# One GpSimd instruction instead of four, and the sample ranks one step earlier

## The chip, the cores and the metric

The kernel runs on one core of one Trainium2 chip. The metric is the device time of one execution in microseconds. The kernel before was timed three times: 759.83, 761.39 and 762.85 us, median 761.39 us.

## The reference

The kernel computes one inference step of one decoder layer in fp32, for a prompt of 256 tokens and for 8 sample sequences of one new token each with 1024 past positions in a paged cache:

```
x = x + 0.5 * g1 * SwiGLU_1(mod1(rmsnorm(x)))
h = mod2(rmsnorm(x)); [qA|kA|vA|qB|kB|vB|gA|gB] = h @ w_in
  A: block-sparse attention, 8 heads x 64, blocks of 256, top 3 past blocks + own block
  B: differential attention, 4 heads, q/k halves of 64, value 128
x = x + g2 * ((sig(gA) * yA + sig(gB) * yB) @ w_out)
x = x + 0.5 * g3 * SwiGLU_2(mod3(rmsnorm(x)))
```

The part that matters here is the attention of the sample group in branch A. Of the four past blocks of a sequence only three take part: those with the highest mean score. Each block's score is compared with the others' (ties go to the lower block), and a block that has three or more ahead of it is masked. After that comes the softmax over the past keys and the new one.

## The kernel before, in words

The 264 tokens (256 + 8) lie along the free dimension, features on the partitions. A weight block is 128 x 2048 floats. Each is split into a high part (a ScalarE copy to the fp32r format, `hi`, L723) and a low part (`lo`: raw minus high, on VectorE at L1069 or on GpSimd at L674), and each product of 128 x 128 is three matmuls (L1626 to L1628). `hi` and `lo` work on halves of a block, 128 x 1024 elements. The order on each engine is written out by hand, and engines meet through semaphores that only count up.

The change lies in the middle stage, from about 290 to 400 us. There the engines run a loop over steps u. At step u:

- TensorE multiplies half u of the weights for keys and values (`kv_product(u)`, halves 0 to 19; halves 16 to 19 belong to the gates), turns the result of the step before (`v_turn`, L1810 and L1811), then multiplies the sample queries with a block of cached keys: `scores(0, u + 2)` and `scores(1, u)`, L1875. Branch A's blocks come through SP's queue (kvA), branch B's through GpSimd's queue (kvB). After step 16 come halves 17 and 18, the turned probabilities (`turn_probs(0)`, L1919), `block_sums(1)`, half 19, and then the products of probabilities and cached values (PV, L2009), whose progress frees the slots for later loads.
- VectorE turns the cached key blocks in place (`turn_keys(ab, u)`, L1280) before TensorE can use them: `turn_keys(0, u + 3)` and `turn_keys(1, u + 1)`. So key block 15 of branch B is turned at its step 14 and used at TensorE's step 15. Between them it has small work: `place_q` (L1299), the products of new queries and keys (`own_products`, L1308), and for sequences of group 0 `sample_logits(0)` (step 10), a copy of the current scores (`ncur`, L1472, step 13), `sample_ranks(0)` (L1337 to L1362, step 14), `prompt_logits(0)` (step 15), `sample_scale(0)` (step 16). Group 1's `sample_ranks(1)` comes after the loop.
- ScalarE copies each product out of its bank (`v_out`, tile vT, L865, and `v_tokens`), cuts the high part of half u + 3, and at its step 14 does `sample_exp(0)` (L880), which waits for the end of `sample_ranks(0)`.
- GpSimd, for each use of a key/value slot of branch B, issues four loads (`kv_load`, L480), which wait until the slot's earlier content has been used, and then cuts the low part of one half (`lo`, halves 5 to 19, fifteen in all). It also stores rows of keys and values (L656, L657).
- `exp_sums(0)` (L1910) on TensorE adds up the exponentials of group 0 over partitions; `sample_scale(0)` waits for it.

SP loads the weight blocks in program order between its own key/value loads; a raw slot is free when the low part of its last half is cut.

Of the kernel before, what the change touches and what calls it, by code (L numbers as in the profile page):

```python
# [16 lines left out]
F32 = mybir.dt.float32  # L17
F32R = mybir.dt.float32r
I32 = mybir.dt.int32
ALU = mybir.AluOpType  # L20
# [5 lines left out]
KC = D // P  # L26
# [186 lines left out]
def build(nc, A, O):  # L213
    ctx = ExitStack()
    with ctx:
# [17 lines left out]
        raw = [place(f"raw{s}", [P, UNIT]) for s in range(SLOTS)]  # L233
        whi = [place(f"whi{s}", [P, UNIT], F32R) for s in range(2)]
        wlo = [place(f"wlo{s}", [P, UNIT], F32R) for s in range(2)]
# [106 lines left out]
        s_hi, s_lo, s_gemm = sem("hi_ready"), sem("lo_ready"), sem("gemm_done")  # L342
# [88 lines left out]
        def half_view(tensor, key, t):  # L431

            n = key[1]
            nk, w = (KC, 256) if W_FF1 <= n < W_DN1 or W_FF2 <= n < W_DN2 else fixed_block(n)[1:]
            return tensor[:, 0:nk * w].rearrange("p (k n) -> p k n", k=nk)[:, :, t * w // 2:(t + 1) * w // 2]
# [196 lines left out]
        @block.gpsimd  # L632
        def _(pool):
            late = CW["dist"][0]
            pool.dma_start(const[:, 0:late], A["consts"][:, 0:late]).then_inc(s_const, 16)

            pool.wait_ge(s_sil, 1)
            pool.dma_start(const[:, late:NCONST], A["consts"][:, late:NCONST]).then_inc(s_const_late, 16)
            pool.wait_ge(s_gemm, half_done(W_DN1 - 1, 1))
            for e in range(2):  # L640
                pool.dma_start(held_ada[e][:, :], ada_src(3, e)).then_inc(s_held[e], 16)
            pool.wait_ge(s_alo, NPAIR)
            for e in range(2, 8):
                pool.dma_start(held_ada[e][:, :], ada_src(3, e)).then_inc(s_held[e], 16)
            pool.wait_ge(s_gemm, half_done(W_QK - 1, 1))
            pool.wait_ge(s_ptab, 16)
            for use in range(KVS + 2):
                kv_load(pool, 1, use)

            def row_out(name, ab, p, src, srcs, done):  # L650
                c0 = 256 * p
                name += ("_moba", "_diff")[ab]
                dst = O[name + "_prompt"][0, 0].rearrange("(a p) h d -> p a (h d)", p=P)[:, :, c0:c0 + 256]
                dsts = O[name + "_sample"][0, :, 0].rearrange("s h d -> s (h d)")[:, c0:c0 + 256]
                f0 = 512 * ab + c0
                pool.dma_start(dst, src[:, :, f0:f0 + 256]).then_inc(done, 16)  # L656
                pool.dma_start(dsts, srcs[:, f0:f0 + 256]).then_inc(done, 16)  # L657

            K_ROWS = {8: 0, 10: 1, 11: 2, 13: 3}
            V_ROWS = {14: 0, 16: 1, 18: 2, 19: 3}  # L660
            pool.wait_ge(s_ada, ADA_N2 + 4)
            for b in range(2):
                ins = nc.gpsimd.memset(qrow[b][:, :, :], 0.0)
            ins.then_inc(s_qzero, 1)
            def lo(n, t):

                key = ("w", n)
                s = slot_of(key)
                pool.wait_ge(s_raw[s], landed(key))
                pool.wait_ge(s_hi, half_done(n, t))  # L670
                pool.wait_ge(s_lo, half_done(n, t) - 1)
                low, full, high = half_view(wlo[n % 2], key, t), half_view(raw[s], key, t), half_view(whi[n % 2], key, t).bitcast(F32)
                for k in range(0, KC, 2):
                    ins = nc.gpsimd.tensor_tensor(low[:, k:k + 2, :], full[:, k:k + 2, :], high[:, k:k + 2, :], ALU.subtract)  # L674
                ins.then_inc(s_lo, 1)

            for use in range(KVS + 2, 4 * TS):
                kv_load(pool, 1, use)
                if 6 <= use <= 11:
                    lo(*filler(use - 1))  # L680
                if 11 <= use < POOL_HALVES - 1:
                    lo(*filler(use))
                if use == POOL_HALVES - 2:
                    lo(*filler(use + 1))
                if use in K_ROWS:
                    i = K_ROWS[use]
                    pool.wait_ge(s_tok, 4 * (i + 1))
                    row_out("k", i // 2, i % 2, ktok, ktoks, s_krow)
                if use in V_ROWS:
                    i = V_ROWS[use]  # L690
                    pool.wait_ge(s_vtok, 4 * (i + 1))
                    row_out("v", i // 2, i % 2, vtok, vtoks, s_vrow)

            def load_last(e):
                pool.dma_start(ada_dst(last_ada[e], ADAS - 1), ada_src(ADAS - 1, e)).then_inc(s_last[e], 16)

            pool.wait_ge(s_pv, 4 * TS)
            load_last(0)
            pool.wait_ge(s_vrow, 16 * 8)
            pool.wait_ge(s_po, KC)  # L700
            load_last(1)
            pool.wait_ge(s_ext, 3)
            load_last(2)
            load_last(3)
# [354 lines left out]
        def _(v):  # L1059
# [378 lines left out]
            for u in range(2 * TS + 2):  # L1438
                if 2 <= u < 18:
                    kind, i = kv_half(u - 2)  # L1440
                    if kind == "k":
                        k_reciprocals(i)
                if u == 2:
                    lo(*filler(4))
                if u % 2 and u + 3 < 16:
                    place_q(0, (u + 3) // 2)
                if u + 3 < 16:
                    turn_keys(0, u + 3)
                if u % 2 and 4 <= u + 1 < 16:
                    place_q(1, (u + 1) // 2)  # L1450
                if u + 1 < 16:
                    turn_keys(1, u + 1)
                if u == 3:
                    for buf in range(2):
                        ins = dve.memset(wpad[buf][:, :, :, :], 0.0)
                    ins.then_inc(s_wzero, 1)
                if u == 10:
                    v.wait_ge(s_kS[1], GUEST_LAST + 1)
                    for e in range(2):
                        for m in mxt[e]:  # L1460
                            ins = dve.memset(m[:, :], 0.0)
                    ch.link(ins)
                    sample_logits(0)
                if u == 11:
                    own_products()
                if u == 12:
                    prompt_q_roots()
                    v.wait_ge(s_mod, ADAS - 1)
                    coefficients(2, R_N3)
                if u == 13:  # L1470
                    v.wait_ge(s_cur, 1)
                    dve.tensor_copy(ncur[:, :], bank[:, 4, 0:4]).then_inc(s_ncur, 1)  # L1472
                if u == 14:
                    v.wait_ge(s_ncur, 1)
                    sample_ranks(0)
                if u == 15:
                    prompt_logits(0)
                if u == 16:
                    sample_scale(0)
# [138 lines left out]
        def _(pe):  # L1618
# [309 lines left out]
            for u in range(2 * TS + 1):  # L1928
                kv_product(u)
                if 1 <= u < 17:  # L1930
                    kind, i = kv_half(u - 1)
                    if kind == "k":
                        k_sum(i)
                    else:
                        v_turn(u - 1, i)
                if 2 <= u < 18:
                    kind, i = kv_half(u - 2)
                    if kind == "k":
                        k_turn(u - 2, i)
                if 3 <= u < 19:  # L1940
                    kind, i = kv_half(u - 3)
                    if kind == "k":
                        k_back(i)
                if u == 5:
                    pe.wait_ge(s_nvar, 3)
                if u == 13:
                    pe.wait_ge(s_ecur, 1)
                    pe.wait_ge(s_kroot, 8)
                    for r4 in range(4):
                        ins = mm(bank[:, 4, r4:r4 + 1], ev0[:, r4, :], C("ones", 0, 1), start=True, stop=True)  # L1950
                    ins.then_inc(s_cur, 1)
                if u + 2 < 16:
                    scores(0, u + 2)
                if u < 16:
                    scores(1, u)
                if u == 11:
                    block_sums(0)
                if u == 14:
                    pe.wait_ge(s_knorm, 8)
                    pe.wait_ge(s_ncur, 1)  # L1960
                    pe.wait_ge(s_part, 1)
                    prompt_scores(0)
                if u == 16:
                    exp_sums(0)

            def gate_half(s, t):
# [182 lines left out]
```

## Time and profile before

| | value |
|---|---|
| time, median of 3 | 761.39 us |
| profiled execution, its own time | 759.83 us |
| its span, first to last instruction | 758.1 us |
| TensorE / VectorE / ScalarE / GpSimd busy | 730.7 / 462.4 / 333.9 / 130.5 us |
| granted TensorE clock, mean | 0.995 |
| HBM traffic over the span | 275 GB/s |

Busy time is the union of an engine's instructions; matmul ends are modelled, so a busy TensorE need not be at its peak. The idle time before an instruction is put down to the engine or transfer whose signal came last.

### The profile page before, as it was taken

How to read it: one execution, taken by the hardware profiler on the slowest of the kernel's cores; microseconds unless marked ns; L12 is line 12 of the kernel's file. 1: busy time of each engine (PE TensorE's matmuls, PEld its weight loads, DVE VectorE, ACT ScalarE, POOL GpSimd, SP SyncE). 2: the span in 40 equal slices, each digit the busy share in tenths (PEclk: the TensorE clock that was granted, in tenths of full speed). 3: DMA queues.
4: the chain of work that ended last, by engine and by line, in shares of the span. 5: the costliest groups of instructions: out<-in, count | busy, mean ns of one | idle time of the engine just before them, and what ended most of it. 6: DMA issues, size and time to landing. Idle time of an engine off the chain costs nothing.

```text
span 758.1 us, 17337 instructions
## 1 busy us (share of the span) xinstructions
PE 730.7 (96%) x6732; PEld 651.7 (86%) x6732; DVE 462.4 (61%) x699; ACT 333.9 (44%) x568; POOL 130.5 (17%) x224
## 2 busy tenths in 40 slices
PE   5899999999999999999989999999989999999997
PEld 2498998999999699999876666599979999999997
DVE  1764445355454779997998555868675545545451
ACT  1553344334343543554345534565463444444431
POOL 0000000002000231797975233110000000000000
PEclk9999999999999999999999999989999999999999
DMA  8978989997995599999999999985616665554620
GB/s 355 377 256 273 321 296 302 335 286 260 401 303 175 213 398 385 360 397 391 406 391 338 408 402 364 361 301 168 207 35 209 186 197 166 173 191 162 200 79 29
DMA packets 116521, 209.57 MB, mean 276 GB/s; under 512 B 6714, under 2 KB 100186, under 8 KB 104162
## 3 DMA queue, kind: packets, MB, share of 16 engines
q1 hardware_dynamic: 106784, 159.47, 60.8%
q0 software_dynamic: 9440, 49.04, 16.4%
q8 instruction: 47, 0.77, 0.4%
q14 instruction: 24, 0.20, 0.1%
q10 hardware_dynamic: 226, 0.10, 0.0%
HBM read 205.33 MB, written 3.24 MB: 275 GB/s over the span
## 4 chain that ended last, share of the span: by engine, by line
PE 79%; DVE 8%; DMA 7%; issue 2%; ACT 2%; SPq 1%; POOL 0%; ACTq 0%; POOLq 0%; DVEq 0%
PE bank L1626 21%; PE bank L1627 20%; PE bank L1628 20%; PE bank L1682 3%; PE bank L1875 3%; DMA raw<-in_w_in 2%; DMA kvA_lent<-in_cache_v_moba 2%; PE bank L2009 2%; DMA kvA<-in_cache_k_moba 1%; PE bank L1690 1%; DMA const<-in_consts 1%; PE bank L1974 1%; SPq L480 1%; DVE wlo L1069 1%; PE bank L1975 1%
## 5 line engine op out<-in xcount | busy, mean ns | idle before, releaser
L1069 DVE TENSOR_TENSOR wlo<-raw,whi 128x1024 fp32r<-128x1024 f32 (+1 forms) x177 | 208.5, 1198 | 175.8 <-ACT whi L723 172.9
L1626 PE MATMUL bank<-hhi,whi 128*128 128x264 f32 x992 | 286.7, 289 | 5.3 <-DVE wlo L1069 2.6
L1627 PE MATMUL bank<-hlo,whi 128*128 128x264 f32 x992 | 282.0, 284 | 0.0
L1628 PE MATMUL bank<-hhi,wlo 128*128 128x264 f32 x992 | 281.6, 284 | 0.0
L723 ACT ACTIVATE whi<-raw 128x1024 fp32r<-128x1024 f32 (+1 forms) x192 | 194.5, 1034 | 111.2 <-PE bank L1628 83.7
L1626 PEld LDWEIGHTS bank<-hhi,whi 128*128 128x128 f32 x992 | 187.6, 189 | 17.8 <-issue 15.0
L1627 PEld LDWEIGHTS bank<-hlo,whi 128*128 128x128 f32 x992 | 187.7, 189 | 0.1
L1628 PEld LDWEIGHTS bank<-hhi,wlo 128*128 128x128 f32 x992 | 186.8, 188 | 0.0
L1626 PE MATMUL bank<-ahi,whi 128*128 128x264 f32 x416 | 119.8, 288 | 0.4 <-DVE alo L1584 0.4
L1628 PE MATMUL bank<-ahi,wlo 128*128 128x264 f32 x416 | 118.2, 284 | 0.0
L1627 PE MATMUL bank<-alo,whi 128*128 128x264 f32 x416 | 117.6, 283 | 0.0
L1626 PEld LDWEIGHTS bank<-ahi,whi 128*128 128x128 f32 x416 | 78.3, 188 | 0.8 <-DVE alo L1584 0.6
L1627 PEld LDWEIGHTS bank<-alo,whi 128*128 128x128 f32 x416 | 78.3, 188 | 0.2
L1628 PEld LDWEIGHTS bank<-ahi,wlo 128*128 128x128 f32 x416 | 78.3, 188 | 0.0
L757 ACT ACTIVATE sil<-bank 128x528 f32<-128x528 f32 x22 | 13.5, 612 | 73.7 <-PE bank L1628 73.7
L674 POOL TENSOR_TENSOR wlo<-raw,whi 128x256 fp32r<-128x256 f32 x60 | 42.8, 744 | 2.9 <-issue 1.4
L761 ACT ACTIVATE ahi<-act 128x528 f32 (+1 forms) x22 | 14.2, 646 | 53.7 <-DVE act L1155 53.7
L480 POOL DMA_DIRECT2D kvB<-in_cache_v_diff x44 | 23.3, 529 | 40.5 <-PE bank L2009 31.8
L1974 PE MATMUL bank<-hhi,whi 128*128 128x264 f32 x96 | 28.5, 297 | 0.0
L1159 DVE TENSOR_TENSOR alo<-act,ahi 128x528 f32 (+1 forms) x22 | 15.6, 708 | 19.4 <-ACT ahi L761 19.4
L1975 PE MATMUL bank<-hlo,whi 128*128 128x264 f32 x96 | 27.3, 284 | 0.0
L1976 PE MATMUL bank<-hhi,wlo 128*128 128x264 f32 x96 | 27.2, 283 | 0.0
(286 smaller groups left out, 814.7 us busy)
## 6 DMA issues: line engine op xcount, KB each, us to landing
raw<-in_ffn_w_gate SPq DMA_DIRECT2D x22, 1024.0 KB, 5.4
raw<-in_ffn_w_up SPq DMA_DIRECT2D x22, 1024.0 KB, 5.5
raw<-in_w_ada SPq DMA_DIRECT2D x20, 1024.0 KB, 6.9
raw<-in_w_in SPq DMA_DIRECT2D x20, 1024.0 KB, 11.9
raw<-in_ffn_w_down SPq DMA_DIRECT2D x16, 1024.0 KB, 5.0
kvB<-in_cache_v_diff POOLq DMA_DIRECT2D x44, 256.0 KB, 6.3
kvA<-in_cache_v_moba SPq DMA_DIRECT2D x40, 256.0 KB, 8.7
kvA<-in_cache_k_moba SPq DMA_DIRECT2D x36, 256.0 KB, 6.7
```

Source lines behind the costliest of these rows:

```text
L480: eng.dma_start(rows_, cache[bass.ds(page, 1)].rearrange("a (j t) d -> (a j) (t d)", t=4)).then_inc(kv_sem(ab, use), 16)
L674: ins = nc.gpsimd.tensor_tensor(low[:, k:k + 2, :], full[:, k:k + 2, :], high[:, k:k + 2, :], ALU.subtract)
L723: nc.scalar.activation(half_view(whi[key[1] % 2], key, t), half_view(raw[s], key, t), ACT.Copy).then_inc(s_hi, 1)
L1069: dve.tensor_tensor(half_view(wlo[key[1] % 2], key, t), half_view(raw[s], key, t), half_view(whi[key[1] % 2], key, t).bitcast(F32), ALU.su ...
L1626: mm(out, wh, xh, start=start, stop=False)
L1627: mm(out, wh, xl, start=False, stop=False)
L1628: return mm(out, wl, xh, start=False, stop=stop)
L1682: ins = mm(bank[32 * j:32 * j + 32, b, 0:n].rearrange("p (t a) -> p t a", a=32), csilu[:, kc, :], cols[:, :, j, :], start=(kc == 0), stop= ...
L1875: ins = mm(bank[32 * m:32 * m + 32, b6, c0:c0 + 128].rearrange("p (q c) -> p q c", q=4), qrow[s % 2][:, 16 * ab + 4 * m + b, :], kv_slot(a ...
L1974: mm(out, wh, hhi[:, k, :], start=(k == 0), stop=False)
L1975: mm(out, wh, hlo[:, k, :], start=False, stop=False)
L1976: ins = mm(out, wl, hhi[:, k, :], start=False, stop=(k == KC - 1))
```

## The change

In GpSimd's `lo`, the loop over four pieces of 128 x 256 elements becomes one instruction over 128 x 1024. On VectorE, `sample_ranks(0)` moves from the start of what step 14 does at its end to the end of step 13, so it now stands ahead of `turn_keys(1, 15)`, which belongs to step 14. On TensorE, `exp_sums(0)` moves from the end of step 16 to the end of step 15, so ahead of `kv_product(16)` and the `v_turn` of half 15.

```diff
-                low, full, high = half_view(wlo[n % 2], key, t), half_view(raw[s], key, t), half_view(whi[n % 2], key, t).bitcast(F32)
-                for k in range(0, KC, 2):
-                    ins = nc.gpsimd.tensor_tensor(low[:, k:k + 2, :], full[:, k:k + 2, :], high[:, k:k + 2, :], ALU.subtract)
-                ins.then_inc(s_lo, 1)
+                nc.gpsimd.tensor_tensor(half_view(wlo[n % 2], key, t), half_view(raw[s], key, t), half_view(whi[n % 2], key, t).bitcast(F32),
+                                        ALU.subtract).then_inc(s_lo, 1)
...
                 if u == 13:
                     v.wait_ge(s_cur, 1)
                     dve.tensor_copy(ncur[:, :], bank[:, 4, 0:4]).then_inc(s_ncur, 1)
-                if u == 14:
                     v.wait_ge(s_ncur, 1)
                     sample_ranks(0)
...
-                if u == 16:
+                if u == 15:
                     exp_sums(0)
```

## Rows read from the trace of the kernel before

**Rows 1.** The page: busy time, share and instructions of each engine; shares of the chain.
```profile
PE 730.7 (96%) x6732; PEld 651.7 (86%) x6732; DVE 462.4 (61%) x699; ACT 333.9 (44%) x568; POOL 130.5 (17%) x224
...
PE 79%; DVE 8%; DMA 7%; issue 2%; ACT 2%; SPq 1%; POOL 0%; ACTq 0%; POOLq 0%; DVEq 0%
```

**Rows 2.** Waits of TensorE, 340 to 426 us: us in total, times, longest.
```profile
PE bank L1810 <- ACT vT L865: 1.5, 1, 1.5
PE bank L1626 <- POOL wlo L674: 1.2, 1, 1.2
PE bank L2009 <- DMA kvA_lent<-in_cache_v_moba: 1.1, 1, 1.1
PE bank L1875 <- DVE kvB L1280: 0.9, 2, 0.7
PE bank L2009 <- ACT wpad L966: 0.2, 1, 0.2
```

**Rows 3.** Windows: length, busy PE, PEld, DVE, ACT, POOL; clock, DMA share, GB/s.
```profile
372.00:396.00 24.00, 21.34 (x241) 19.42 (x242) 21.60 (x52) 10.04 (x27) 20.80 (x32) 1.00 1.03 400
400.00:408.00 8.00, 8.00 (x97) 3.92 (x90) 7.43 (x20) 3.14 (x12) 4.10 (x8) 1.00 0.81 262
```

**Rows 4.** The chain that ended last, 366 to 412 us: start, us, what.
```profile
377.16 18.67 DMA raw<-in_w_in
...
397.86 0.58 ACT probT L887
```

**Rows 5.** Timeline of VectorE: start, us, instruction, count, idle before and its releaser.
```profile
357.85 1.75 DVE L1299 TENSOR_TENSOR qrow<-qrep,const 128x32 f32<-128x32 f32 x2
...
361.71 0.28 DVE L1299 TENSOR_TENSOR qrow<-qrep,const 128x32 f32<-128x32 f32 x2
...
364.11 1.61 DVE L1308 TENSOR_TENSOR stat<-qT,kT 128x32 f32<-128x32 f32 x2
...
374.52 0.12 DVE L1472 COPY ncur<-bank 128x4 f32<-128x4 f32 x1
375.82 2.31 DVE L1280 STREAM_TRANSPOSE kvB<-kvB 128x2048 f32<-128x2048 f32 x1 [1.18 <-DMA kvB<-in_cache_k_diff]
378.06 0.13 DVE L1337 COPY sm<-bank 128x8 f32<-128x8 f32 x1
...
379.77 0.75 DVE L1350 TENSOR_SCALAR sm<-sm,const 128x8 f32<-128x8 f32 x1
...
382.99 0.54 DVE L1357 TENSOR_TENSOR mxt<-mxt,ncur 128x2 f32<-128x2 f32 x1
...
384.52 0.16 DVE L1362 TENSOR_TENSOR ncur<-ncur,mxt 128x2 f32<-128x2 f32 x1
...
395.62 0.17 DVE L1337 COPY sm<-bank 128x8 f32<-128x8 f32 x1
...
400.20 0.16 DVE L1362 TENSOR_TENSOR ncur<-ncur,mxt 128x2 f32<-128x2 f32 x1
```

**Rows 6.** Timeline of ScalarE, columns as in rows 5.
```profile
384.72 0.51 ACT L880 ACTIVATE prob<-prob,mxt 128x256 f32<-128x256 f32 x1 [6.55 <-DVE ncur L1362]
```

**Rows 7.** Timeline of GpSimd, three of the fifteen low halves.
```profile
356.60 2.80 POOL L674 TENSOR_TENSOR wlo<-raw,whi 128x256 fp32r<-128x256 f32 x4
...
374.89 2.80 POOL L674 TENSOR_TENSOR wlo<-raw,whi 128x256 fp32r<-128x256 f32 x4
...
381.07 3.13 POOL L674 TENSOR_TENSOR wlo<-raw,whi 128x256 fp32r<-128x256 f32 x4
```

**Rows 8.** The page, groups: busy us, mean ns of one; VectorE's low parts.
```profile
L1069 DVE TENSOR_TENSOR wlo<-raw,whi 128x1024 fp32r<-128x1024 f32 (+1 forms) x177 | 208.5, 1198 | 175.8 <-ACT whi L723 172.9
```

**Rows 9.** Timeline of TensorE: scores(1, 15) and the first matmul of half 18.
```profile
380.59 1.08 PE L1875 MATMUL bank<-kvB,qrow 128*32 128x128 f32 x32
...
391.11 0.36 PE L1626 MATMUL bank<-hhi,whi 128*128 128x264 f32 x1 [1.20 <-POOL wlo L674]
```

**Rows 10.** Window, columns as in rows 3.
```profile
494.00:504.00 10.00, 9.78 (x53) 9.55 (x54) 4.53 (x9) 5.62 (x10) 2.15 (x3) 0.66 0.96 361
```

## The prediction, made before the changed kernel ran

> **What bounds the kernel now.** I read the page first: TensorE is busy 730.7 of 758.1 us, and the chain that ended last is TensorE's for 79% [rows 1]. So a change in the other engines counts only where TensorE stands still. The second view is the list of waits between 340 and 426 us: TensorE loses 1.5 us to a copy on ScalarE (vT), 1.2 us to a low half from GpSimd, 0.9 us in two waits for a turned key block, 0.2 us for the padded weights and 1.1 us for a transfer [rows 2]. These are all the gains that this stretch can give. The third view, the windows, shows who is short of time there: from 372 to 396 us VectorE is busy 21.6 of 24 us and the DMA engines are full (share 1.03); from 400 to 408 us their share falls to 0.81 [rows 3]. The chain of waits passes this place not through TensorE at all, but through an 18.67 us transfer of input weights that lands at 395.83 us, two copies on ScalarE and the turned probabilities at 397.86 us [rows 4].
>
> The 1.5 us wait arises so. VectorE's copy of the current scores is done at 374.6 us; then it waits 1.18 us for the last key block, turns it, and only from 378.06 to 384.68 us ranks the blocks [rows 5]. ScalarE stands 6.55 us before its exponential [rows 6], and the copy vT of half 15 is queued behind that. GpSimd's low half 18 needs ScalarE's high half 18, which is queued there too; from that comes the 1.2 us.
>
> **VectorE: the ranks go ahead of the last key block.** Nothing is added. The ranks can start at 374.66 us instead of 378.06. Alone they take 395.62 to 400.36 = 4.74 us, as the second use shows [rows 5], against 6.62 us in the first use, beside GpSimd. Moved forward, they meet two low halves of GpSimd, which start at 374.89 and 381.07 us [rows 7]. What such a meeting costs is in two rows: a pair of VectorE multiplies of 32 elements, started at 357.85 us in the second of GpSimd's four pieces (356.60 us, 2.80 us in all), ended only after the fourth, 1.75 us later, where the same pair takes 0.28 us at 361.71; the two products at 364.11 us took 1.61 us in the same way [rows 5, 7]. L1357, at 382.99 us, took 0.54 us, where L1362, of the same size, takes 0.16: there the wait ended with the current piece. Both happen with four pieces; with one piece only the long wait is possible.
>
> The Trainium skill, "SBUF — State Buffer", section "Who interferes with whom", states that a VectorE instruction with two SBUF inputs contends with a GpSimd instruction that reads SBUF, and that the first holds the port for its whole instruction. By that rule the four pieces let VectorE in every 0.7 us and the single one does not: a rule against this change. The trace agrees for L1357 and not for the row at 357.85 us, which outlasted two piece ends; the sum below is the same by either.
>
> **GpSimd: one instruction for four.** Fifteen low halves (60 pieces). The price of one at 128x1024 is in no row: 2.79 us for the four pieces bounds it above, VectorE's 1.2 us for the same shape below [rows 7, 8]. I take 2.5 us, near the four-piece row, because engine and data are those; only start-up can go. Saving: 0.3 us each. GpSimd is waited for by TensorE only once, at half 18, but VectorE waits for the end of a low half twice on its way to TensorE (357.85 and 364.11 us [rows 5]), so key blocks come 0.3 and then 0.6 us earlier. Of the 0.9 us that TensorE waits there [rows 2] I count 0.6 us (bounds 0 and 0.9).
> The Trainium skill, "GPSIMD Engine Reference", section 3.1, has about 2.6 cycles per element at 1.2 GHz for this operation, an estimated 2.2 us for 1024; with it the upstream gain would be the full 0.9 us and each hold 0.3 us shorter.
>
> **The ranks' new end.** Start 374.66, plus 4.74 alone, plus 2.3 us because L1345 (at 375.07) meets the first low half until 377.4, plus 0.5 us since L1350, which took 0.75 us beside GpSimd's descriptor work, meets that again [rows 5]: 382.2 us. The next low half starts at 380.8 (381.07 less the 0.3 saved) and ends at 383.3; it catches L1362, the last operation (end 383.5 us), or already L1357 (end 384.6 us). I take 384.0 us. Without any hold it is 379.4; with 2.8 us per hold and the earlier catch 385.2.
>
> **TensorE: what then waits.** Behind the ranks stands the turn of key block 15, 2.31 us [rows 5]; it ends at 386.3 us. TensorE needs it for scores(1, 15), which started at 380.59 us [rows 9]. It is queued in order: everything behind it (the exponential sums, halves 16 to 19, all PV products) stands too. New wait: 386.35 - 380.59 = 5.8 us. The 0.6 us from upstream move VectorE, GpSimd and TensorE alike and come off once: +5.2 us.
> The sums moved from step 16 to 15 cost nothing: ScalarE's exponentials take 1.1 us after the ranks (two of 0.51 [rows 6] and a small one), so they are ready at 385.1 us, before the scores end (the cover is that very wait; without it TensorE would stand up to 1.1 us less the scores' 1.0).
> Given back: vT 15 is ready long before, and so is the high half 18: the waits of 1.5 and 1.2 us go [rows 2]. GpSimd's next key/value load waits for scores(1, 15), until 386.8 us, and low half 18 stands behind it; TensorE needs that at 393.6, 6.8 us later, and a whole round of GpSimd (row stores, loads and a low half) takes 381.07 - 374.89 = 6.2 us [rows 7]. Balance at half 18: 5.2 - 2.7 = +2.5 us over 391.11 [rows 9].
> From there: the 0.2 us before the PV products is absorbed (+2.3). VectorE comes 1 to 3 us later into logits, scale and second ranks and meets low halves 18 and 19 there; with 21.6 of 24 us busy [rows 3] it has little to spare: 0 to 0.8 us, I take 0.4. SP's value loads follow the PV products, so the thin DMA stretch at 400 to 408 us moves along and hides little; of the 1.1 us wait at 424 us I take 0.3 as hidden. Sum: 2.3 + 0.4 - 0.3 = **+2.4 us**. After it the kernel is bound by TensorE, and nothing gives it back.
>
> The profiled execution took 759.83 us for its span of 758.1; +2.4 makes a span of 760.5 and 762.2 us. It was the fastest of three, 1.56 us under the median of 761.39: so **763.8 us**.
>
> **Rivals.** (a) *The clock falls.* TensorE would stand nearly 6 us. After the thin stretch up to 494 us the granted clock fell to 1.2 GHz: mean 0.66 over 494 to 504 us, that is 10 x 0.34 = 3.4 us lost if the work is dense [rows 10]. The stretch of dense products behind the new wait would pay that. For: no stop of 1.5 us in this trace lowered it, but this one is four times as long. Against: that row's fall came after many small matmuls, no single stop. Price 1.7 to 3.4 us, mean 2.6: 766.4 us.
> (b) *Not slower: VectorE slips between the low halves.* If the ranks end before 380.9 us, the key block is turned by 383.2 and the 2.7 us given back cover the wait; that is where the sign turns at half 18. Fully free they end at 379.4, TensorE arrives 1.1 us early there, 1.7 with the upstream gain. But the PV products then meet ScalarE, whose queue waits for the weight transfer that lands at 395.83 us, with the DMA engines full [rows 3, 4], and whose weights TensorE waits for even now, 0.2 us [rows 2]. So the gain shrinks to 0 to 0.2 us: 761.2 us. For: L1357's short wait. Against: the long waits of small two-input operations.
> (c) *The ranks' cost is passed on worse*: both ends of 385.2 us and 0.8 us on VectorE, nothing hidden: +4.3, 765.7 us. This is my case's upper end, not a case of its own.
>
> **How the numbers follow.** The forecast's own range is +1.0 to +4.3 us, 762.4 to 765.7. Chances: forecast 0.48, (a) 0.27, (b) 0.22, something unforeseen 0.03. Half a per cent, about what a measurement of this kernel can tell, is 3.8 us: 757.6 and 765.2 are the borders. The forecast lies within by 0.9 of its chance, (a) by 0.25, (b) by nearly all: within 0.43 + 0.07 + 0.20, less some for luck of the median, 0.67; slower 0.28; faster 0.05. The range has to hold (b) and most of (a): 760.2 to 767.6.
>
> **What would show it.** L674 fifteen times at about 2.5 us (2.2 to 2.8). L1345 or L1344 at over 2 us. ScalarE's exponential no longer behind a 6.55 us wait after 378 us, the 1.5 us wait for vT gone. A new TensorE wait of 5 to 6 us ahead of the L1875 scores of kvB, released by VectorE's L1280; then half 18 without a wait for L674. A granted clock under 1.00 between 380 and 396 us means (a). Ranks that end before 381 us mean (b), with more than 0.2 us of wait for wpad before the PV products. I am wrong if that TensorE wait is under 3 us, or if the PV products do not shift with it.

## The result and the profile after

The changed kernel is slower: 766.95 us median of 14 runs (763.12 to 768.29) against 761.1 us of the kernel before, timed beside it. The ratio on record is 1.0062 with a 95% interval of 1.0047 to 1.0078, about 4.7 us; the two medians of 14 differ by more, 5.85 us, while the 35 executions on record of the changed kernel have a median of 766.15 us. The forecast of 763.8 us was too low; the time fell near rival (a), 766.4 us. The profiled execution has a span of 763.0 us.

The page after: busy times, and the group of GpSimd's low halves, now fifteen instructions.
```profile
PE 731.7 (96%) x6732; PEld 652.5 (86%) x6732; DVE 467.1 (61%) x699; ACT 334.5 (44%) x568; POOL 123.6 (16%) x179
...
L672 POOL TENSOR_TENSOR wlo<-raw,whi 128x1024 fp32r<-128x1024 f32 x15 | 35.8, 2386 | 3.1 <-ACT whi L721 2.8
```
GpSimd saved 7 us of busy time (42.8 to 35.8), and nothing of it reached the end. VectorE is busy 4.7 us longer with the same number of instructions, because some of them lasted longer: they were held.

TensorE's waits from 372 to 430 us were 1.5, 1.2, 1.1 and 0.2 us before [rows 2]. After, one above all:
```profile
PE bank L1872 <- DVE kvB L1278: 7.0, 1, 7.0
```

VectorE's timeline after shows what made it (columns as in rows 5; line numbers are 2 lower):
```profile
374.40 0.12 DVE L1470 COPY ncur<-bank 128x4 f32<-128x4 f32 x1
...
374.98 2.75 DVE L1343 TENSOR_TENSOR rank<-sm 128x32 f32<-128x32 f32 x1
...
378.92 4.77 DVE L1352 TENSOR_TENSOR prob<-prob,sm 128x256 f32<-128x256 f32 x2
...
385.58 0.16 DVE L1360 TENSOR_TENSOR ncur<-ncur,mxt 128x2 f32<-128x2 f32 x1
385.66 2.31 DVE L1278 STREAM_TRANSPOSE kvB<-kvB 128x2048 f32<-128x2048 f32 x1
```
GpSimd beside it:
```profile
375.30 2.38 POOL L672 TENSOR_TENSOR wlo<-raw,whi 128x1024 fp32r<-128x1024 f32 x1
...
378.89 2.13 POOL L480 DMA_DIRECT2D kvB_lent<-in_cache_v_diff  x4
381.05 2.35 POOL L672 TENSOR_TENSOR wlo<-raw,whi 128x1024 fp32r<-128x1024 f32 x1
```
The ranks take 374.55 to 385.74 us, 11.2 us for work of 4.7. An operation of 0.19 us lasted 2.75, to the end of the first low half. The pair L1352, 0.89 us alone, lasted 4.77, to the end of the second; its second member began at 379.38 us, 1.7 us before that low half is recorded as started.

TensorE and its clock (timeline; then windows: length, busy PE, PEld, DVE, ACT, POOL, clock, DMA share, GB/s):
```profile
388.02 1.94 PE L1872 MATMUL bank<-kvB,qrow 128*32 128x128 f32 x32 [6.95 <-DVE kvB L1278]
```
```profile
384.00:388.00 4.00, 0.00 (x0) 0.00 (x0) 3.79 (x9) 2.22 (x9) 0.00 (x0) 0.50 1.01 420
388.00:394.00 6.00, 5.98 (x51) 5.50 (x52) 5.65 (x16) 0.61 (x1) 2.90 (x5) 0.52 1.06 356
400.00:408.00 8.00, 8.00 (x92) 5.78 (x94) 5.33 (x20) 3.78 (x9) 0.66 (x2) 1.00 0.53 167
490.00:515.00 25.00, 23.71 (x166) 18.31 (x165) 19.14 (x40) 17.48 (x32) 2.88 (x4) 0.93 0.98 351
```
TensorE did nothing from 384 to 388 us, the clock fell to 1.2 GHz, and the same scores took 1.94 us and not 1.08 [rows 9]. From the start of these scores to the first PV product TensorE needed 398.83 - 380.59 = 18.2 us before, 2.9 of them waits; after it needed 405.46 - 388.02 = 17.4 us with no wait. So 15.3 us of work took 17.4: 2.1 us are the clock's.

The account of the stretch: wait 6.95, less the 2.9 returned, plus 2.1 = 6.2 us. The first PV product moved by 6.6 us, 0.4 of which the two executions already differed by at 371 us. In this pair of executions 1.6 us came back near 500 us. There the clock fell for less long: over 490 to 515 us its mean was 0.93, and 0.86 in the kernel before, that is 25 x 0.07 = 1.75 us. (Rows 10 do not compare directly: the work of the changed kernel comes 6 us later.) That varies from execution to execution: the three other kernels with a wait of 6.2 to 7.0 us have 0.86, 0.93 and 0.80 over the same window. The DMA share in 400 to 408 us sank from 0.81 to 0.53, so transfers did not bind there.

### The profile page after: what moved, and what is told of

It is laid out like the page before. It is cut to its first block, busy times and chain, and to the rows that moved or that the text cites. A ratio compares the mean times of both kernels' runs of the same rounds, so it can differ in the third digit from the quotient of the medians.

```text
span 763.0 us, 17292 instructions
## 1 busy us (share of the span) xinstructions
PE 731.7 (96%) x6732; PEld 652.5 (86%) x6732; DVE 467.1 (61%) x699; ACT 334.5 (44%) x568; POOL 123.6 (16%) x179
## 4 chain that ended last, share of the span: by engine, by line
PE 78%; DVE 10%; DMA 6%; issue 2%; ACT 2%; SPq 1%; ACTq 0%; DVEq 0%
PE bank L1623 22%; PE bank L1624 21%; PE bank L1625 21%; DMA early<-in_w_ada 3%; PE bank L1872 3%; DMA kvA_lent<-in_cache_v_moba 2%; PE bank L1679 2%; PE bank L2006 2%; DMA kvA<-in_cache_k_moba 1%; DVE wlo L1067 1%; PE bank L1971 1%; DVE kvB L1278 1%; PE bank L1972 1%; PE bank L1973 1%; DVE prob L1352 1%
## 5 line engine op out<-in xcount | busy, mean ns | idle before, releaser
L672 POOL TENSOR_TENSOR wlo<-raw,whi 128x1024 fp32r<-128x1024 f32 x15 | 35.8, 2386 | 3.1 <-ACT whi L721 2.8
```

The lines of the kernel that those rows point to most:

```text
L672: nc.gpsimd.tensor_tensor(half_view(wlo[n % 2], key, t), half_view(raw[s], key, t), half_view(whi[n % 2], key, t).bitcast(F32), ALU.subtra ...
```

## The parts of the change, one at a time

All kernels below were timed in five rounds beside the kernel before; ratios are to it.

**GpSimd's single instruction alone** (the change's first hunk; ranks and sums as before).

> Only GpSimd's single instruction; the ranks and the sums stand as before. Theory (the reorder costs, the single instruction only saves 0.4 us per low half): the wait for low half 18 before TensorE's half 18 shrinks from 1.2 to about 0.8 us, but the PV products start when ScalarE's copies behind the weight transfer allow, so the time is that of the kernel before within 0.3 us (ratio 0.999 to 1.001), no wait of TensorE over 2 us, and the clock stays at 1.00 from 375 to 400 us. Rival (the long hold of the port by the single instruction costs by itself): VectorE's small two-input operations wait longer, the ranks' 6.6 us become 8 us or more, the wait for vT 15 grows from 1.5 to 3 us, and the kernel is 1 to 3 us slower.

Measured: 1.0021 (1.0005 to 1.0037), 1.6 us slower. The rival was right: the ranks take 8.3 us (377.68 to 386.01 us). VectorE's timeline shows three holds, the first over GpSimd's descriptors and the low half behind them; TensorE's waits follow:
```profile
378.96 3.80 DVE L1347 TENSOR_SCALAR sm<-sm 128x8 f32<-128x8 f32 x1
...
389.11 2.30 DVE L1393 SCALAR_TENSOR_TENSOR stat<-stat,qroot 128x2 f32<-128x2 f32 x1
...
391.71 2.26 DVE L1370 TENSOR_SCALAR sm<-sm,misc 128x2 f32<-128x2 f32 x1
```
```profile
PE bank L1808 <- ACT vT L863: 3.1, 1, 3.1
PE bank L1903 <- DVE prob L1327: 0.9, 1, 0.9
```
The wait for low half 18 is gone, but that for vT 15 has doubled, since the ranks end later. The expectation that the clock would stay up failed as well. After the stop of 3.09 us it fell here too (window of this kernel):
```profile
388.00:392.00 4.00, 4.00 (x22) 4.00 (x22) 3.83 (x7) 3.86 (x11) 2.82 (x2) 0.57 1.01 397
```
That is at most 4 x 0.43 = 1.7 us of dense work, so a part of what this edit costs is also the clock's. No run separates it from the longer waits.

**The moves alone** (low halves in four pieces as before; the diff is the change's second and third hunk).

> The ranks and the sums moved as in the change, GpSimd's low half in four pieces as before. Theory (the reorder costs, with either form of the low half, because an operation held at the first piece is often held to the last): L1345 of the ranks takes over 2 us, TensorE's wait for key block 15 is 6 to 7.5 us, the clock falls, and the time is that of the changed kernel or up to 1 us longer (low halves are 0.4 us longer): ratio to before 1.006. Rival (the pieces let VectorE in every 0.7 us, the single instruction does not): the ranks are 1.5 to 3 us shorter than in the changed kernel, TensorE waits 4 to 5 us, and the kernel is at 1.002 to 1.004 of before.

Measured: 1.0055 (1.0035 to 1.0075). The theory's case: the ranks take 10.6 us. VectorE's timeline and TensorE's wait:
```profile
374.72 2.91 DVE L1344 TENSOR_TENSOR rank<-sm 128x32 f32<-128x32 f32 x1
...
379.65 3.01 DVE L1354 TENSOR_TENSOR prob<-prob,sm 128x256 f32<-128x256 f32 x2
...
383.42 0.52 DVE L1357 TENSOR_TENSOR mxt<-mxt,ncur 128x2 f32<-128x2 f32 x1
```
```profile
PE bank L1874 <- DVE kvB L1280: 6.8, 1, 6.8
```
The first operation was held past all four pieces, as at 357.85 us before [rows 5]. The pair at L1354 ended at 382.66 us, inside the second low half (four pieces from 380.96 to 383.92 us): there VectorE got in between the pieces. L1357 took 0.52 us, to the end of the last piece, after which none followed. The ranks end 0.7 us earlier than with the single instruction. The parts cost 4.2 and 1.6 us alone and 4.7 together; their sum is not distinguishable from that.

**The exponential sums back at step 16** (six timings).
```diff
-                if u == 15:
+                if u == 16:
                     exp_sums(0)
```


> The changed kernel with the exponential sums of group 0 back at step 16, so only GpSimd's single instruction and the moved ranks are left of the change. Theory (the sums' place costs and brings nothing, since the exponentials are ready before the scores of key block 15 end): the time of the changed kernel within 0.5 us, ratio to before 1.005 to 1.007, TensorE's wait for key block 15 again about 7 us. Rival (the early sums let VectorE's scale start earlier and are worth something): VectorE's scale starts 3.5 us later and the kernel is 1 us or more slower than the changed one, ratio 1.0075 or above.

Measured: 1.0066 (1.0047 to 1.0086), as the changed kernel. The move of the sums does nothing that can be measured.

## What the port and the clock are worth

**Low halves 16 and 17 cut.** The order of the changed kernel, GpSimd's reads beside the ranks taken away: 31 of 32 elements of these two low parts are left out.
```diff
+                if (n, t) in (filler(16), filler(17)):
+                    low, full, high = low[:, :, 0:4], full[:, :, 0:4], high[:, :, 0:4]
```


> The changed kernel, but low halves 16 and 17 on GpSimd are cut to 4 of 128 columns in each row block (the rest of these two low parts is left out, so 31 of 32 of their elements are stale). This takes GpSimd's reads away beside the first ranks. Theory (the port is what stretches the ranks from 4.7 to 11 us): the ranks take 4.7 to 5.5 us, TensorE's wait for key block 15 is 0.5 to 2 us, the clock stays at 1.00, and the time is within 0.5 us of the kernel before, not faster by more than that, since the PV products then wait for ScalarE behind the weight transfer. Rival (the order alone costs, the port little): the ranks still take over 8 us and TensorE waits over 4 us.

Measured: 1.0011 (0.9991 to 1.003). The ranks run from 373.97 to 378.90 us, 4.9 us; TensorE waits 0.7 us for the key block. So GpSimd's two low halves are shown as what stretches them from 4.9 to 11.2 us; that they do it through a port shared with VectorE is not shown by itself. And the reorder, even so, gains nothing: TensorE comes early to the PV products and waits for ScalarE's padded weights, and ScalarE stands 6.69 us behind the weight transfer (waits of TensorE; timeline of ScalarE):
```profile
PE bank L2008 <- ACT wpad L966: 3.6, 1, 3.6
PE bank L1874 <- DVE kvB L1280: 0.7, 1, 0.7
```
```profile
396.73 2.00 ACT L723 ACTIVATE whi<-raw 128x1024 fp32r<-128x1024 f32 x2 [6.69 <-DMA raw<-in_w_in]
```
That is rival (b) of the prediction, played out.

**The same, and ScalarE's queue reordered.**
```diff
             gate_pair(0)
-            for t in range(2):
-                hi(W_GATE + 2, t)
             turned_probs(0)
...
             gate_pair(1)
+            for t in range(2):
+                hi(W_GATE + 2, t)
```


> The changed kernel with the low halves 16 and 17 cut to 4 of 128 columns per row block (the rest of them left out) and ScalarE's two high halves of gate block 2 behind the padded weights. It shows what the reorder would be worth with no hold of the port and no ScalarE wait. Theory: the 3.6 us wait for wpad that the kernel with cut low halves had goes, the PV products start near 396 us, and 1 to 3 us of it reach the end: ratio 0.996 to 0.999. Rival (the transfers bind this stretch: the DMA engines are full until 400 us): the 3.6 us come back as waits for key/value transfers within the next 40 us, ratio 1.000 or above.

Measured: 0.9963 (0.9941 to 0.9984), 2.8 us faster than before. The wait for wpad is gone, and the transfers take back only 0.8 us. So they did not bind the stretch in the kernel with cut low halves; the order of ScalarE's queue did.

**TensorE kept busy while it waits.**
```diff
+FILL = 13
...
+                if u == 15:
+                    pe.wait_ge(s_vtok, 2 * (kv_half(12)[1] + 1))
+                    for _ in range(FILL):
+                        mm(bank[:, 0, 0:256], C("ones"), const[:, 0:256], start=True, stop=True)
```


> The changed kernel with 13 extra matmuls of 128 x 256 (about 5.6 us of work, results overwritten) on TensorE just before it waits for key block 15. Theory (the wait of 7 us also lowers the clock, and that costs 2 to 3 us of the 6): the wait proper shrinks to 0.5 to 1.5 us, the granted clock stays at 1.00 from 380 to 400 us, and the kernel is 2 to 3 us faster than the changed one, so 1.002 to 1.004 of before. Rival (only the wait costs; the dense products have slack enough for the lower clock): the time is that of the changed kernel, 1.006.

Measured: 1.0031 (1.0012 to 1.005), against 1.0062 of the changed kernel timed beside other runs: about 2.4 us less. The clock stayed at 1.00 (window of this kernel, then of the changed one):
```profile
380.00:396.00 16.00, 14.66 (x125) 13.39 (x125) 15.35 (x27) 4.95 (x15) 8.98 (x10) 1.00 1.04 396
```
```profile
380.00:396.00 16.00, 9.05 (x78) 8.25 (x77) 15.38 (x27) 3.42 (x12) 7.90 (x8) 0.68 1.04 394
```
The results of the added matmuls are overwritten; they only fill time in which TensorE would have waited, and still the kernel is faster. It agrees with the 2.1 us counted in the trace. The two intervals overlap a little, so the size is rough, and only the timings show it: the profiled execution's span, 763.6 us, is not below the 763.0 of the changed kernel, whose fall near 500 us was shorter (0.93 against 0.86 over 490 to 515 us).

**The low half ahead of the loads at use 17.**
```diff
+                if use == 17:
+                    lo(*filler(use))
                 kv_load(pool, 1, use)
```


> The changed kernel, but at use 17 GpSimd cuts its low half before it issues the four loads, so the low half stands behind two store descriptors and not behind six descriptors. Theory (a low half that is queued behind descriptor writing holds the port already from then on, 1 to 2 us before its recorded start): the low half is recorded near 378.9 to 381.3 us, the second of the ranks' operations that it held (4.3 us in the changed kernel) shrinks to under 3 us and ends with it, the ranks end 1.5 to 2.5 us earlier, TensorE waits 4.5 to 5.5 us for key block 15 and not 7. Rival (the hold comes from the descriptors themselves): an operation is still held through the four loads, past 383 us, and the wait stays at 7 us. The time by the first: 1 to 2 us less than the changed kernel, ratio 1.004; by the second 1.006.

Measured: 1.0051 (1.0029 to 1.0073), not to be told from the changed kernel. The trace moved as the theory says, by less than it said. VectorE, then GpSimd:
```profile
377.15 2.77 DVE L1345 TENSOR_TENSOR rank<-sm 128x32 f32<-128x32 f32 x1
...
380.18 3.36 DVE L1347 TENSOR_TENSOR rank<-rank 128x32 f32<-128x32 f32 x1
```
```profile
379.79 0.76 POOL L656 DMA_DIRECT2D out_v_moba_prompt<-vtok  x1
380.55 0.52 POOL L657 DMA_DIRECT2D out_v_moba_sample<-vtoks  x1
381.09 2.40 POOL L672 TENSOR_TENSOR wlo<-raw,whi 128x1024 fp32r<-128x1024 f32 x1
```
The hold begins 0.9 us before the low half's recorded start (1.7 us with four loads more ahead of it) and ends with it, at 383.5 us; the four loads after it hold nothing of this kind. TensorE waits 6.2 us. I had asked for under 3 us of hold and 4.5 to 5.5 us of wait; both were missed, because the operation was still held from 0.9 us ahead of the record to its end, 3.3 us in all. "GPSIMD Engine Reference" of the Trainium skill, section 2.1, has the cores of GpSimd each go on to the next instruction once their own share is done, and section 4 has a pair of them write descriptors; idle cores that already read for the low half would look like this. No run here shows the cores.

## Where the returned 2.7 us go

**ScalarE's exponential one step later**, in the kernel before: it removes the waits of 1.5 and 1.2 us with nothing else moved.
```diff
-                if u == 14:
+                if u == 15:
                     sample_exp(0)
```


> The kernel before with one edit on ScalarE: the exponential of group 0 stands at the end of its step 15 and not 14, so vT 15 and high half 18 no longer wait behind the ranks. This gives TensorE the 1.5 and 1.2 us that the change was credited with, without moving the ranks. Theory (that gain is worth nothing, because the PV products wait for ScalarE behind the weight transfer that lands near 396 us): both waits are gone, a wait of 2 to 3 us for wpad comes up before the PV products, and the time is within 0.5 us of before (ratio 0.999 to 1.001). Rival (the PV products can start earlier, the 2.7 us are real): ratio 0.9965 to 0.998, wait for wpad under 1 us.

Measured: 1.0008 (0.9983 to 1.0033), no difference, as the theory says, but not by its road. Only 0.4 us is waited for wpad; the rest comes up earlier, at the sums that wait for VectorE and ScalarE:
```profile
PE bank L1910 <- ACT ncur L882: 2.0, 1, 2.0
PE bank L1905 <- DVE prob L1329: 1.1, 1, 1.1
```

**The same, with ScalarE's two high halves behind the padded weights** (the move of `hi(W_GATE + 2, t)` shown above).

> As the kernel with the later exponential, and ScalarE's two high halves of gate block 2 (which wait for the weight transfer) stand behind the padded weights and not ahead of the turned probabilities. Theory (the order of ScalarE's queue, not the transfer's data, holds the PV products): they start 1 to 2.7 us earlier than before; part of it is then lost to the exponential sums of group 1 (VectorE, 1 to 2 us) and to the value loads; ratio 0.997 to 0.9995. Rival (the PV products then wait for their own transfers or for VectorE as long): ratio 0.9995 to 1.001, with a wait of 1.5 us or more in the first 10 us of the PV products.

Measured: 0.9998 (0.9977 to 1.0019): the rival. TensorE now waits 1.3, 0.8 and 1.1 us for the exponentials, for the scale and for the second logits. VectorE's chain of ranks, logits and scale is as short of time here as TensorE is.

## A version that beats both

If GpSimd's low halves beside the ranks are the cost, these two belong to VectorE, which takes its instructions one after the other. Nothing of the computation changes.
```diff
-                if 11 <= use < POOL_HALVES - 1:
+                if 11 <= use < POOL_HALVES - 1 and use not in (16, 17):
                     lo(*filler(use))
...
                     dve.tensor_copy(ncur[:, :], bank[:, 4, 0:4]).then_inc(s_ncur, 1)
+                    v.wait_ge(s_lo, half_done(*filler(16)) - 1)
+                    lo(*filler(16))
                 if u == 14:
                     v.wait_ge(s_ncur, 1)
                     sample_ranks(0)
+                    v.wait_ge(s_lo, half_done(*filler(17)) - 1)
+                    lo(*filler(17))
```
and ScalarE's two high halves moved as above.

> The order of the kernel before, four pieces on GpSimd, but low halves 16 and 17 on VectorE: the first in its 1.2 us of idle time ahead of key block 15, the second behind the ranks; ScalarE's two high halves of gate block 2 behind the padded weights. Nothing of the computation changes. Theory (the port's hold is the cost, the ranks' place is right): the ranks take 4.7 to 5.0 us and not 6.6, TensorE's waits for vT 15 and low half 18 go, waits for VectorE (sums of the second group) of 1 to 2 us remain; ratio 0.9965 to 0.9995. Rival (VectorE's time is what is short here, and two more low halves of 1.2 us eat what the port gives back): ratio 0.9995 to 1.001.

Measured: 0.9973 (0.9954 to 0.9992), 759.6 us median, 2.1 us faster than before, with the ranks where they were:
```profile
376.15 1.21 DVE L1069 TENSOR_TENSOR wlo<-raw,whi 128x1024 fp32r<-128x1024 f32 x1
377.27 2.30 DVE L1280 STREAM_TRANSPOSE kvB<-kvB 128x2048 f32<-128x2048 f32 x1
379.50 0.13 DVE L1337 COPY sm<-bank 128x8 f32<-128x8 f32 x1
...
384.04 0.16 DVE L1362 TENSOR_TENSOR ncur<-ncur,mxt 128x2 f32<-128x2 f32 x1
```
The low half of 1.21 us fills the 1.18 us that VectorE stood before key block 15 [rows 5], and the ranks take 4.7 us. ScalarE's move is a part of this version; low halves on VectorE without it were not timed.

**With the change's order and its single instruction** (low halves 16 and 17 on VectorE behind key block 15, same ScalarE order).

> The changed kernel (ranks ahead of key block 15, single instruction on GpSimd), but low halves 16 and 17 on VectorE behind key block 15, and ScalarE's two high halves of gate block 2 behind the padded weights. It is the correct sister of the kernel with the two cut low halves, which was 0.9963 of before. Theory: the ranks take 4.7 to 5.2 us, TensorE waits 0.7 to 1.5 us for key block 15 and a little for low half 16, the clock stays up; VectorE is 2.4 us later than in that kernel, so 1 to 2 us of its gain remain: ratio 0.9975 to 0.9995. Rival (VectorE short): 1.000 or above, with 2 us or more of waits for it between half 16 and the PV products.

Measured: 0.9979 (0.9965 to 0.9993). Waits of TensorE: 1.1 us for the key block, 1.1 and 0.4 for VectorE's logits and scale. Not distinguishable from the version above: with no low half of GpSimd beside them, these runs show no difference by the ranks' place.

**With block_sums(1) behind half 19** added to the first of the two.
```diff
             turn_probs(0)
-            block_sums(1)
             kv_product(19)
+            block_sums(1)
```


> As the kernel with low halves 16 and 17 on VectorE, and on TensorE block_sums(1) stands behind half 19 and not ahead of it, since it waited about 1 us for VectorE in each kernel that was early there. Theory: that wait goes and 0 to 1 us reaches the end: ratio 0.9955 to 0.999. Rival: the second ranks then start later and the wait comes back at the exponential sums of group 1 (2 us or more there): the same time as its sibling or up to 0.5 us slower.

Measured: 1.001 (0.9997 to 1.0023). The rival, and stronger than it: the second ranks start later, and TensorE waits 2.5 us for the exponentials of group 1:
```profile
PE bank L1914 <- ACT ncur L882: 2.5, 1, 2.5
```

## Why the prediction was right, and where not

**The mechanism.** Right: the ranks ahead of key block 15 make TensorE wait for it, VectorE is held twice by GpSimd's low halves, and the time rises. Cutting the two low halves takes the holds away and leaves 0.7 us of the wait.

**The single instruction's price.** Taken 2.5 us, measured 2.39 us.

**The upstream gain.** Taken 0.6 us; the two waits before 372 us sum to 0.8 us after and 0.9 before. Low half 13 began 0.8 us later than before (357.39 against 356.60 [rows 7]), as GpSimd's loads ahead of it wait for TensorE's scores, so VectorE was held to 359.8 us, not earlier. A faster low half only waits longer at the next load.

**The ranks' end.** Forecast 384.0 us, measured 385.74. The first hold was 2.6 us (taken 2.3); the second was the mis-sized term. I let the second begin with the low half's record and end the ranks one or six operations later; it began 1.7 us earlier, at L1352, so all the operations behind it, 2.0 us, came after the hold.

**TensorE's wait and what is returned.** Forecast 5.8 us, 5.2 after the upstream gain; measured 6.95 us. The returned 2.7 us were right, and the 0.2 too.

**The clock.** This step failed as a choice: I gave the fall 0.27 against 0.48 and took the forecast without it. The fall is in the trace of the change, and its price, forecast 2.6 us, is 2.1 in the trace and about 2.4 by the kernel that fills the wait. All four profiled executions with a wait of 6.2 to 7.0 us show it: their mean clock from 380 to 400 us is 0.74, 0.83, 0.74 and 0.74, and 1.00 with the wait filled. Over the whole execution the granted clock averages 0.987 in the 35 of the changed kernel, 0.991 in the 99 on record of the kernel before, and 0.992 in the twelve timed with the filled wait. The two executions of the changed kernel at 0.993 are at 763.12 and 763.7 us. A mean over a whole execution does not say where the clock fell, so whether it falls here every time stays open.

**VectorE's knock-on and the DMA's cover.** Taken +0.4 and -0.3 us. After the long wait TensorE waited for VectorE nowhere (0), and the wait at the value transfer shrank from 1.10 to 0.96 us (0.1).

**Rival (b).** Its claim that TensorE's lead would end at ScalarE behind the weight transfer is shown by the cut kernel (3.6 us of wait, ratio 1.0011). But with a lead of only 2.7 us, VectorE's sums come first.

**Part of the cost I had on the wrong edit.** I priced the single instruction as a gain of 0.3 us each and no cost of its own; alone it costs 1.6 us.

**What was luck.** With the terms as the trace has them the sum is 6.95 - 2.9 + 2.1 - 0.1 = 6.05 us at the value transfer, not 2.4. The 1.6 us that came back near 500 us stand in no term and bring it to 4.5, close to rival (a)'s 5.0. So (a) met the time in part because two misses cancel: a wait that was 1.75 us longer than the net one I took, and the 1.6 us returned. My case's own range ended at 765.7 us, below the measured median; only the range widened for the rivals holds it. I had also given 0.67 to a change within half a per cent and 0.28 to "slower"; it was slower, by 0.62%.

## What to carry to other kernels

Beside another engine's long instruction a small operation can cost the whole rest of that instruction and, as here, of what is queued for it; before moving a chain of such operations look for rows that are many times as long as their like (2.75 us against 0.19). An in-order engine's idle time is not free to use: what stands behind the moved work is late by all that the move picks up on the way. A wait of TensorE (3.1 and 7.0 us here) can have a second price, the clock, which shows only in windows of the granted clock; and a wait removed is a gain only when the next releaser in that engine's order is early too.

## What the runs showed of the hardware that I had not expected

- A hold begins before GpSimd's instruction is recorded: 1.7 us before, with six descriptor instructions ahead of it, 0.9 us with two. Spans on GpSimd are rough in the record; the holds end within 0.3 us of the recorded end of the low half.
- VectorE's one-input TENSOR_SCALAR of 8 elements was held too, for 3.80 us, not only operations with two inputs.
- Four pieces of 0.7 us let VectorE in at one time and not at another, in the same run: in the kernel before L1357 took 0.54 us (0.16 alone) and ended with the third piece at 383.5 us, with the fourth still to come, and the pair at 357.85 us was held through to the end of the fourth.
- A stop of TensorE of 3.09 us was followed by 1.2 GHz (0.57 over 388 to 392 us, single instruction alone); stops of 1.5 us in the kernel before were not (1.00).
